# Issuing the down-projection loads of a mixture-of-experts stage from ScalarE's queue

## The reference

```
for each block of up to 64 rows, of one expert e:
    gu = xb @ w_gate_up[e] + b_gate_up[e]         # (64, 1024) @ (1024, 2048)
    gl, up = split(gu, 2)
    act = min(gl, 7) * sigmoid(1.702 * gl) * (clip(up, -7, 7) + 1)
    y = act @ w_down[e] + b_down[e]               # (64, 1024) @ (1024, 1024)
out[token] = sum over its four experts of gate * y[row of the token]
```

## Time and profile before

| | us |
|---|---|
| median of three runs | 1825.71 |
| the profiled execution | 1825.03 |
| its span, first to last instruction | 1823.30 |
| PE busy in the span | 1508.8 (83%) |
| DVE busy | 608.7 (33%) |
| POOL busy | 294.0 (16%) |
| ACT busy | 245.0 (13%) |
| granted TensorE clock, mean | 0.913 of 2.4 GHz |

### The profile page before, as it was taken

The page is one execution under the profiler, slowest core; times in us unless marked ns, Lnnn a source line. Parts: engine busy times, 40 slices in busy tenths (PEclk is TensorE's granted clock), DMA queues, the critical chain, the costliest instruction groups (busy, mean ns, idle before and its releaser), DMA issues.

```text
span 1823.3 us, 19309 instructions
## 1 busy us (share of the span) xinstructions
PE 1508.8 (83%) x6894; PEld 793.9 (44%) x6894; DVE 608.7 (33%) x1072; ACT 245.0 (13%) x502; POOL 294.0 (16%) x308
## 2 busy tenths in 40 slices
PE   7899976998998969998888788788887888788870
PEld 2788865644885656333222232222323232232320
DVE  0462679759537548111111011111111111011115
ACT  1322320121132122000000000000000000000001
POOL 1000038237105100011001010010101001010105
PEclk9899988899988976989999989999999999999985
DMA  9556321155150452999999999999999999999975
GB/s 339 205 189 156 113 88 47 47 183 187 47 185 0 200 216 93 371 402 409 403 407 400 411 408 406 410 406 410 403 411 408 404 410 404 411 406 407 409 300 190
DMA packets 121416, 533.35 MB, mean 293 GB/s; under 512 B 10592, under 2 KB 11104, under 8 KB 87072
## 3 DMA queue, kind: packets, MB, share of 16 engines
q1 hardware_dynamic: 112992, 506.58, 71.3%
q0 software_dynamic: 7168, 21.90, 3.5%
q10 hardware_dynamic: 1216, 4.33, 0.6%
HBM read 508.23 MB, written 24.54 MB: 292 GB/s over the span
## 4 chain that ended last, share of the span: by engine, by line
PE 39%; DMA 22%; SPq 17%; DVE 16%; issue 3%; ACT 2%; POOL 1%; ACTq 0%; DVEq 0%; POOLq 0%
DMA ring<-gate_up_dram 21%; SPq L378 16%; PE ps L419 13%; PE ps L741 7%; DVE cvT L1118 5%; PE ps L722 5%; PE ps L430 3%; PE ps L603 1%; PE ps L731 1%; PE ps L682 1%; DVE hT L1435 1%; DVE AS L1437 1%; DVE hT L1430 1%; DVE hT L1432 1%; PE ps L528 1%
## 5 line engine op out<-in xcount | busy, mean ns | idle before, releaser
L722 PE MATMUL ps<-ring,XS 128*64 128x512 f32 x2112 | 494.6, 602 | 90.8 <-DMA ring<-gate_up_dram 90.5
L741 PE MATMUL ps<-work,AS 128*64 128x512 f32 x1056 | 284.3, 700 | 60.3 <-DVE AS L1437 60.3
L722 PEld LDWEIGHTS ps<-ring,XS 128*64 128x64 f32 x2112 | 138.0, 137 | 441.2 <-DMA ring<-gate_up_dram 232.5
L419 PE MATMUL ps<-hT,ring 128*128 128x264 f32 x1024 | 239.2, 393 | 0.0
L419 PEld LDWEIGHTS ps<-hT,ring 128*128 128x128 f32 x1024 | 198.3, 195 | 34.7 <-issue 0.5
L1424 DVE COPY G<-ps 128x512 f32<-128x512 f32 x33 | 22.8, 692 | 539.9 <-PE ps L722 524.6
L741 PEld LDWEIGHTS ps<-work,AS 128*64 128x64 f32 x1056 | 84.4, 160 | 235.8 <-issue 170.9
L1118 DVE SCALAR_TENSOR_TENSOR cvT<-uP,pv,cvT 128x256 f32<-128x256 f32 x180 | 137.4, 833 | 0.0
L1539 POOL COPY idxc<-tabi 64x1 int32 (+1 forms) x34 | 6.6, 194 | 659.3 <-PE ps L707 604.5
L1419 DVE COPY gcol<-tabg 128x1 f32 (+1 forms) x33 | 5.1, 154 | 306.8 <-ACT qT L991 306.4
L430 PE MATMUL ps<-ring,cT 128*9 128x512 f32 x192 | 85.9, 601 | 12.4 <-DMA ring<-ada_dram 9.6
(11 more groups left out here) (346 smaller groups left out, 1431.5 us busy)
## 6 DMA issues: line engine op xcount, KB each, us to landing
ring<-gate_up_dram SPq DMA_DIRECT2D x264, 1024.0 KB, 22.6
work<-down_dram SPq DMA_DIRECT2D x132, 1024.0 KB, 24.2
ring<-in_dram SPq DMA_DIRECT2D x16, 2048.0 KB, 10.6
ring<-ada_dram SPq DMA_DIRECT2D x12, 2048.0 KB, 8.1
yrows_dram<-qT POOLq DMA_DIRECT2D x66, 128.0 KB, 5.6
yrows_dram<-S SPq DMA_DIRECT2D x1, 4096.0 KB, 20.6
ring<-pw_dram SPq DMA_DIRECT2D x2, 2048.0 KB, 7.7
ring<-out_dram SPq DMA_DIRECT2D x2, 2048.0 KB, 8.4
```

What stands on the lines that cost most here:

```text
L419: mm = pe.matmul(ps[:, n % 2, 0:cols], ring[:, j % RING, k, (n % CPB) * P:(n % CPB + 1) * P], rhs[:, k, 0:cols], start=(k == 0), stop=(k = ...
L722: mm = pe.matmul(ps[CAP * s:CAP * (s + 1), n, :], XS[:, i, :], raw(i)[:, s * D + n * BW:s * D + (n + 1) * BW], start=(i == 0), stop=(i == ...
L741: mm = pe.matmul(ps[CAP * n:CAP * (n + 1), 4, :], AS[:, 2 * (i - GU) + a, :], raw(i)[:, a * D + n * BW:a * D + (n + 1) * BW], start=(i == ...
```

## The change

The helper `load` moves out of SP's program and takes the engine that starts the transfer. SP's loop keeps the eight gate/up units of a block. ACT's `body` starts the four down units of its block, right behind `rows_of` for the preceding block. ACT's wait there is for the last of that block's units; before, SP waited for each down unit by itself. In the overflow loop ACT now reads the block's expert number from `obi` too. Block 0's units are loaded by SP as before. Buffers, semaphores, sizes and the arithmetic are the same.

```
+        def load(eng, e, i):
+            if i < GU:
+                src, dst = wgu[e, :, i, :], raw(i)
+            else:
+                src, dst = wdn[e, :, i - GU, :, :], work[:, 2 * (i - GU):2 * (i - GU) + 2, :]
+            eng.dma_start(dst, src).then_inc(raw_in[i], 16)
...
             def body(blk, e):
-                for i in range(UNITS):
+                for i in range(GU):
                     sp.wait_ge(unit_used, UNITS * blk - UNITS + i + 1)
-                    load(e, i)
+                    load(sp, e, i)
...
             def body(blk, e):
                 if not isinstance(blk, int):
                     rows_of(blk - 1)
+                    for i in range(GU, UNITS):
+                        load(act, e, i)
                 act.wait_ge(unit_used, UNITS * blk + GU)
...
-            n = overflow(act, body)
+            n = overflow(act, lambda blk, b: body(blk, act.value_load(obi[0:1, bass.ds(b, 1)], min_val=0, max_val=E - 1)))
```

More of the change, by code:

```diff
@@ L312, in build @@
                 + [("chunk", n) for n in range(C_GDN, C_GDN + CPB)])
+        wgu = A["gate_up"].rearrange("e (k p) n -> e p k n", p=P)
+        wdn = A["down"].rearrange("e (u a p) n -> e p u a n", p=P, a=2)
+        def load(eng, e, i):
[4 more added lines that the diff above has]
+            eng.dma_start(dst, src).then_inc(raw_in[i], 16)
         wd = par("w_dw").rearrange("p (k j) -> p k j", j=CC)
@@ L368, in _ @@
             sp.dma_start(qT[:, :, :], A["xT"]).then_inc(in_x2, 16)
[L370 to L378, removed]
             for i in range(GU):
                 sp.wait_ge(chunk_done, CPB * (NB - RING + i // 2 + 1))
-                load(0, i)
+                load(sp, 0, i)
             sp.wait_ge(out_st, 6 * 16)
```

## The result

The changed kernel takes 1892.74 us (median; 1890.21 to 1895.13) against 1826.31 us before (four runs; the 1825.71 of the table above is the median of three of them): 1.0364 times as long, 95% interval 1.0346 to 1.0382, so 66 us slower. The forecast was slower, by 161 us. The way was right, the size two and a half times too large.

What follows compares the result with a forecast made beforehand. DMA was taken to bound late expert blocks at 32.2 us. Block 0 ending at 758.45, 31 blocks at 37.1 and a last of 27.8 end the stage 161.7 later: 1825.03 becomes 1987 us, range 1830 to 2120.

Steps and rivals of the forecast that it cites:

- Who shares the engines: DMA engines in the expert stage: one packet from each queue in turn, so 4 KB down rows get a third of the bytes.
- equal bytes: Rival for the two weight queues: equal shares, down units land in time, blocks stay at 32.2 us; 1825 to 1832 us; chance 0.14.
- Mixing costs no bandwidth: Two weight queues keep the full rate; the rival, loss by mixing, gave 2259 us, chance 0.16 wholly or in part.
- Issuing: ACT's four transfer starts per block, 1.3 to 2.1 us, fit its idle time and cost nothing; SP's relief gains nothing.
- When the down units start: All four are issued 0.1 to 0.8 us after PE's end of the preceding block; 0.8 taken.
- The lone stretch: At each block's start the down queue is alone about 0.9 us (6 packets), then 58 packets alternate with gate/up for 27.2 us.
- The sum: Fourth down unit lands 33.6 to 35.1 us after the preceding block's end; each of 31 blocks takes 37.1 us.
- The last block: End of the expert stage: no next gate/up units beside it, down units land within about 15 us, it takes PE's 27.8.
- The range: Whole kernel, for eight in ten: from the equal-bytes case, 1830, up to a partial loss by mixing, 2120 us.
- its main case: Whole kernel, down queue getting a third of the bytes: 1931 to 2021 us, most likely 1987; chance 0.60.
- the signs named ahead: PE waits for down units several us a block, 37 us block windows, DMA share below 1, packets one to one.

## Why the prediction was right in kind and wrong in size

*Who shares the engines: right.* The term that decides was read from the earlier trace rows, on POOL's queue, and holds for ACT's: 305 packets to 303, by turns of one packet. The Trainium skill's "DMA: Bandwidth & Descriptors", section "Queues, rings and completion order", has an engine drain a packet of typically 9 to 17 descriptors before it turns; here the turns are one row long, and equal bytes came about only when the rows were made equal. The prediction's step from that rule to equal bytes was itself loose: it needs turns of one transfer's share, 8 rows of the one queue and 16 of the other, while turns of one number of rows for both queues give a third of the bytes, however long they are.

*Mixing costs no bandwidth: right.* 419 GB/s in the shared stretch. The slow rate of the earlier trace rows stayed with the gather.

*Issuing: right.* ACT's four issues took 2.06 us from 1307.14, and L1002, at 1321.80, came when PE's sums were ready.

*When the down units start: off by half a microsecond.* ACT's first transfer was issued at 1307.14, 0.3 us after PE's end, not 0.8: ACT issued while its eviction ran, from 1307.00 to 1307.69.

*The lone stretch: the step that failed.* The prediction said that "the down queue is alone for about 0.9 us (6 packets, 0.96 us), then 58 packets alternate". In the short block shown it is alone from 1308.16, its first row, to 1313.41, the refill's first: 5.2 us, in which 414 rows pass, 26 of the 64 on each engine (the window shown above has 375 of them, its 391 packets less 16 tiny ones). In all 16 short blocks it is 23 to 27. In the 15 long blocks it is 0 to 7: only they are as the sum had it. The timeline shows where the 4.3 us come from (start us, length us):

```profile
1306.65 15.10 PE L723 MATMUL ps<-ring,XS 128*64 128x512 f32 x64
1307.14 2.06 ACTq L322 DMA_DIRECT2D work<-down_dram  x4
1309.92 41.49 SPq L322 DMA_DIRECT2D ring<-gate_up_dram  x16
```

PE comes out of a wait at the lower clock level (0.64 granted on the mean from 1306.9 to 1309.9), and its first gate/up unit takes 3.05 us (1306.87 to 1309.92), not 1.72: 1.3 us. ACT's issue is the half microsecond earlier. And the refill's first row appears 3.5 us after its issue, while the down queue's, on idle engines, appears 1.0 us after its own: 2.5 us, where the sum had given both the same delay. The four transfers' landings, min, median and max us from issue, in the short and in the long block:

```profile
DMA to landing us min/median/max: 5.1/13.7/24.3
```

```profile
DMA to landing us min/median/max: 10.4/21.4/32.4
```

The fourth down unit of the short block thus lands at 1308.74 + 24.3 = 1333.0, 26.2 us after the block's start, and PE, slowed by the lower clock, comes to it at 1335.3: no wait (in others of the short blocks up to 2.1 us). Twenty rows more than the six of the sum pass without a gate/up row of 0.309 us beside each, which is 6.2 us of the difference to the 33.6 to 35.1 worked out. In the long block it is 34.2, inside them. What differs is what the block before left behind. A long block ends with the engines idle and the gate/up queue empty, so the next down units run alone first. A short block ends while gate/up units are still coming in (the last of them lands 5 us later), so the next down units meet them: their first row appears 3.5 us after the issue, and they are alone for 1.2 us at most a little later, when those units have passed and the refill's first row has not come.

*The sum: one term mis-sized.* "31 blocks at 37.1" were 16 short ones of 29.7 on average and 15 long ones of 38.7, together 31 of 34.04 (757.74 to 1813.04 us): 31 × 3.06 = 95 us of the 161.7 did not come. The last block and everything around the stage were nearly as reckoned: the stage ended 67.6 us later than before, and the profiled execution took 66.9 us more (1891.91 less 1825.03). The two runs that take the lone stretch away and lengthen it, 2093 and 1846 us, show that it carries this difference.

*The range was wide enough by luck, the centre wrong.* The prediction treated a block as if each began in the same state. The low end of its main case, 1931, was worked out from a fixed lone stretch; no bound was put on the stretch itself. The measured 1893 lies below that case, and within the range only because the range reached down to the equal-bytes rival, which did not happen. Of the signs named ahead PE's waits, the DMA share and the one-to-one packets held; the block windows show 30 and 38 us, not 37.

## What to carry to other kernels

Two queues that kept the same DMA engines busy added no bandwidth here, they set an order: each got packets in turn, so the queue with the shorter rows got the fewer bytes. A transfer that is needed soon must not be started late there. Where one queue in the order of use keeps the engines full, leave it, and look at the row length instead. When a step's time depends on what the step before left in a queue, work out two steps in a row, not one.

## What the runs showed that was not expected

A first row appears 1.0 to 1.1 us after its issue on idle engines (ACT's in the 16 short blocks) and 3.0 to 4.4 us after it with another queue at work (ACT's in the long blocks, SP's refill in the short ones). The fold's weight loads of 128x128 float32, read with a step of two elements, took 209 ns instead of 141. And a later request can be a gain: refilling three gate/up units up to 5 us later took 47 us off the changed kernel.
